# Second rates one slab earlier, the last sums inside the last slab, reloads in parts on SP, two slab copies of each turn on ACT: the RWKV projections of a hybrid diffusion step

## The reference

```python
xx = 0.5 * (prev + nxt) - h
xs = h[:, :, None, :] + xx[:, :, None, :] * p['rwkv_mu'][j]
rkvg = jnp.einsum('bsmd,mde->bsme', xs[:, :, :4], p['rwkv_w_in'][j])     # r, k, v, g
lw = decay0 + einsum(tanh(xw @ decay1), decay2)      # two directions
icl = sigmoid(icl0 + einsum(xa @ icl1, icl2))        # two directions
k_dir = k[:, :, None] * (1.0 + (icl - 1.0) * p['rwkv_k_a'][j])
bonus = (sum over a head of (r * k_dir * r_k)) * v, summed over the two directions
out = ((y + bonus) * silu(g)) @ p['rwkv_w_out'][j]   # y: the scan, a later phase
```

## Time and profile before

| what | value |
|---|---|
| median of 3 runs | 5470.27 us (5454.3 to 5471.65) |
| the profiled execution | 5479.65 us |
| its span | 5477.9 us |
| granted TensorE clock, mean | 0.919 |
| busy share of the span | PE 84%, PEld 71%, DVE 47%, ACT 35%, POOL 7% |

### The profile page before, as it was taken

One profiled execution on the slowest core, in us unless ns is written; L12 is line 12 of the kernel. 1 busy time (PEld: TensorE's weight loads), 2 busy tenths in 40 slices (PEclk: granted clock), 3 DMA queues, 4 the chain that ended last, 5 costly groups with the idle time before them and its releaser, 6 DMA issues. The chain is left out here.

```text
span 5477.9 us, 151392 instructions
## 1 busy us (share of the span) xinstructions
PE 4581.2 (84%) x68388; PEld 3876.7 (71%) x68388; DVE 2569.9 (47%) x4055; ACT 1943.1 (35%) x3694; POOL 362.7 (7%) x134
## 2 busy tenths in 40 slices
PE   3799868898887869888888599878998689889966
PEld 0488758888885745446667499876887588888846
DVE  0542436766664323136664432326324476667642
ACT  0542223444445123136663200026422244444441
POOL 0011100000000100000001022110111000000001
PEclk7899988999989879989999799989999899989988
DMA  9134573322226000000000011112446632323251
GB/s 405 44 113 134 153 201 107 85 79 77 80 75 148 31 30 27 27 6 1 1 1 28 16 43 42 35 57 69 121 124 175 202 88 71 84 71 84 62 150 58
DMA packets 624676, 466.63 MB, mean 85 GB/s; under 512 B 27456, under 2 KB 600256, under 8 KB 619712
## 3 DMA queue, kind: packets, MB, share of 16 engines
q1 hardware_dynamic: 451200, 370.05, 22.1%
q10 hardware_dynamic: 172864, 87.30, 5.7%
HBM read 333.28 MB, written 123.99 MB: 83 GB/s over the span
## 5 line engine op out<-in xcount | busy, mean ns | idle before, releaser
L417 PE MATMUL ps<-big_r,stage_r 128*128 128x384 f32 x3072 | 625.8, 338 | 95.9 <-DVE big_r L404 89.7
L623 PE MATMUL ps<-big_r,stage_r 128*128 128x384 f32 x2976 | 646.0, 352 | 25.9 <-DVE big_r L842 25.9
L417 PEld LDWEIGHTS ps<-big_r,stage_r 128*128 128x128 f32 x3072 | 546.0, 190 | 104.8 <-issue 89.4
L623 PEld LDWEIGHTS ps<-big_r,stage_r 128*128 128x128 f32 x2976 | 530.1, 191 | 105.4 <-issue 55.0
L1175 PE MATMUL ps<-arena 64*64 64x32 f32 x11520 | 438.6, 226 | 19.3 <-issue 17.8
L396 POOL TENSOR_TENSOR w_slab_r<-w_slab,stage_r 128x1024 fp32r<-128x1024 f32 x64 | 192.1, 3002 | 3763.2 <-DVE stage_r L380 3763.2
L1175 PEld LDWEIGHTS ps<-arena 64*64 64x64 f32 x11520 | 403.1, 143 | 29.8 <-issue 22.1
L417 PE MATMUL ps<-big_r,w_slab_r 128*128 128x384 f32 x1536 | 351.3, 336 | 0.0
L623 PE MATMUL ps<-big_r,w_slab_r 128*128 128x384 f32 x1488 | 344.7, 339 | 0.0
L368 PE MATMUL ps<-arena,w_slab 128*128 128x384 f32 x864 | 294.3, 502 | 27.0 <-DVE arena L1849 24.1
L1489 DVE COPY_PREDICATED arena<-arena,ps 128x128 f32<-128x128 uint32 x720 | 193.9, 325 | 183.0 <-PE ps L1149 181.8
(11 more groups left out here) (209 smaller groups left out, 7791.6 us busy)
## 6 DMA issues: line engine op xcount, KB each, us to landing
w_slab<-in_w SPq DMA_DIRECT2D x150, 512.0 KB, 3.5
scan_in<-x_resid ACTq DMA_DIRECT2D x112, 576.0 KB, 4.9
arena<-in_w_ada SPq DMA_DIRECT2D x24, 2048.0 KB, 27.8
arena<-scan_in SPq DMA_DIRECT2D x144, 320.0 KB, 3.8
arena<-scan_in SPq DMA_DIRECT2D x288, 128.0 KB, 3.8
arena<-scan_in SPq DMA_DIRECT2D x144, 192.0 KB, 4.0
arena<-scan_in SPq DMA_DIRECT2D x44, 576.0 KB, 7.8
arena<-scan_in ACTq DMA_DIRECT2D x36, 576.0 KB, 10.9
```

What stands on the lines that cost most here:

```text
L417: mm = pe.matmul(g.ps[:, bank + c, 0:CW], w[:, k * P:(k + 1) * P], x[:, k, c * CW:(c + 1) * CW], start=k == i == 0, stop=k == NB - 1 and i ...
L623: mm = pe.matmul(g.ps[:, 3 * s + c, 0:CW], w[:, k * P:(k + 1) * P], x[:, k, chunk(c)], start=k == i == 0, stop=k == NB - 1 and i == 2)
```

## The change

The icl rates of block b + 1 move from gate slab 27 + b to gate slab 26 + b, so the first gate slab holds rates(9) (after k-blocks 3, 5 and 7) and the last gate slab none. The sums of the blocks 6 and 7 both stand inside the last gate slab. The product buffer is doubled (`prod`, one of them `kk[1]`). The reloads all go to SP, k and r apart from v, the first two as soon as their part of `xx` is free. DVE's `products` is split: the sum of the two rates (`rate_sums(b)`) goes ahead, and the rest stands behind the slab copy. At each turn the copies of the first two slabs of the new matrix go from DVE to ACT (`turn`, `high_slab_of` on ACT).

```diff
-    prod = g.big[0][:, 0, :]
+    prod = [kk[1], g.big[0][:, 0, :]]
-    rates_in.update({GATE + b: NB + b for b in range(1, NB)})
+    rates_in.update({GATE + b: NB + b + 1 for b in range(NB - 1)})
...
+            def load_kr(b):
+                sp.wait_ge(stored[b % 2], 16 * (5 + b // 2))
+                if b >= 2:
+                    sp.wait_ge(p_ok, b - 1)
+                else:
+                    sp.wait_ge(xs_ok, 3 * NB + 3 * b + 2)
+                for k, arr in enumerate((A_K, A_R)):
+                    sp.dma_start(tiled(back[b % 2][k]), blocks(b, arr)).then_inc(kr_in[b % 2], 16)
+            def load_v(b):
+                sp.wait_ge(stored[b % 2], 16 * (9 + b // 2))
+                if b >= 2:
+                    sp.wait_ge(bonus_ok, CH * (b - 1))
+                else:
+                    sp.wait_ge(xs_ok, 3 * NB + 3 * b + 3)
+                sp.dma_start(tiled(back[b % 2][2]), blocks(b, A_V)).then_inc(v_in[b % 2], 16)
...
                 elif n > GATE:
                     b = n - GATE
+                    if b + 1 < NB:
+                        load_kr(b + 1)
                     store_gate(b - 1)
+                    if b + 1 < NB:
+                        load_v(b + 1)
                     store_bonus(b - 1)
...
+                    at = (3, 5, 7) if n == GATE else (1, 3, 5)
+                elif n == W_RWKV - 1:
+                    between = {j_: (lambda q=NB - 2 + i // CH, c=i % CH: sums(q, c),) for i, j_ in enumerate((1, 2, 3, 5, 6, 7))}
...
+            def high_slab_of(n):                      # on ACT
+                act.wait_ge(slab_in[n % 2], 16 * (n // 2 + 1))
+                act.wait_ge(proj_done, n - 1)
+                A.copy(g.stage_r[:, n % 2, 0:D], g.slab[:, n % 2]).then_inc(turn_ok, 1)
+            def turn(m):
+                high_slab_of(first[m])
+                for k in range(NB):
+                    high_rows(m, k)
...
+            high_slab_of(GATE + 1)
+            for b in range(NB):
+                if b < NB - 1:
+                    for c in range(CH):
+                        rates(NB + b + 1, c)
                 gate(b)
-                if b + 1 < NB:
-                    act.wait_ge(bonus_ok, CH * b)
-                    for i, arr in enumerate((A_K, A_R, A_V)):
-                        act.dma_start(tiled(back[(b + 1) % 2][i]), blocks(b + 1, arr)).then_inc(back_in[(b + 1) % 2], 16)
...
                 if m == 5:
                     if b:
-                        products(b - 1)
+                        rate_sums(b)
+                    weighted_keys(b)
+                    if b:
                         gated(b - 1)
                         high_slab_of(n + 1)
+                    products(b)
+                    if b:
                         for c in range(CH):
                             bonuses(b - 1, c)
-                    weighted_keys(b)
```

More of the change, by code:

```diff
@@ L566, in _ @@
                 if n == GATE:
[L567 to L571, removed]
+                    for b in range(2):
+                        load_kr(b)
+                        load_v(b)
                 elif n > GATE:
                     b = n - GATE
+                    if b + 1 < NB:
+                        load_kr(b + 1)
                     store_gate(b - 1)
+                    if b + 1 < NB:
+                        load_v(b + 1)
                     store_bonus(b - 1)
+            store_bonus(NB - 1)
             store_gate(NB - 1)
-            store_bonus(NB - 1)
             for s in range(2):
@@ L664, in sums @@
                 bank_free(("sum", b, c))
-                pe.matmul(g.ps[:, bank(("sum", b, c)), 0:CW], g.head_ones[:, :], prod[:, chunk(c)], start=True, stop=True).then_inc(sum_mm, 1)
+                pe.matmul(g.ps[:, bank(("sum", b, c)), 0:CW], g.head_ones[:, :], prod[b % 2][:, chunk(c)], start=True, stop=True).then_inc(sum_mm, 1)
             lora_down(0)
@@ L678, in _ @@
                 elif n in rates_in:
-                    between = {j_: (lambda u=rates_in[n], c=c: rates(u, c),) for c, j_ in enumerate((1, 3, 5))}
+                    at = (3, 5, 7) if n == GATE else (1, 3, 5)
+                    between = {j_: (lambda u=rates_in[n], c=c: rates(u, c),) for c, j_ in enumerate(at)}
                     if n > GATE:
                         between.update({j_: (lambda q=n - GATE - 1, c=c: sums(q, c),) for c, j_ in enumerate((2, 4, 6))})
+                elif n == W_RWKV - 1:
+                    between = {j_: (lambda q=NB - 2 + i // CH, c=i % CH: sums(q, c),) for i, j_ in enumerate((1, 2, 3, 5, 6, 7))}
                 slab(n, m, between)
-            for c in range(CH):
-                sums(NB - 1, c)
         @block.scalar
@@ L772, in _ @@
                 if b == NB - 1:
-                    for k in range(NB):
-                        high_rows(3, k)
+                    turn(3)
                 elif b:
@@ L783, in _ @@
                 elif b == NB - 1:
-                    for k in range(NB):
-                        high_rows(4, k)
+                    turn(4)
                 elif b:
@@ L789, in _ @@
                 copy_out(RCP + b)
+            high_slab_of(VAL + 1)
             for b in range(NB):
                 if b == NB - 1:
-                    for k in range(NB):
-                        high_rows(5, k)
+                    turn(5)
                 elif VAL + b in rates_in:
@@ L812, in _ @@
             for n in range(KEY + 1, W_RWKV):
-                pool.wait_ge(high_ok, n - 2)
+                turned = [first[m] + i for m in (3, 4, 5) for i in range(2)]
+                if n in turned:
+                    pool.wait_ge(turn_ok, turned.index(n) + 1)
+                else:
+                    pool.wait_ge(high_ok, n - KEY - sum(t < n for t in turned))
                 nc.gpsimd.tensor_tensor(g.slab_r[:, n % 2], g.slab[:, n % 2], g.stage_r[:, n % 2, 0:D], op=ALU.subtract).then_inc(low_ok, 1)
@@ L855, in transition @@
             def transition(m, extra):
-                n = first[m]
                 rows_of(m, 0)
@@ L946, in _ @@
                     high_slab_of(n + 1)
+                if n == VAL + NB - 2:
+                    dve.wait_ge(kk_st[1], 64)
+                    rate_sums(0)
                 if KEY < n < RCP or n == RCP + 1:
@@ L956, in _ @@
                     dve.wait_ge(xx_ok, NB)
-            products(NB - 1)
-            gated(NB - 1)
             for c in range(CH):
                 bonuses(NB - 1, c)
+            gated(NB - 1)
             dve.wait_ge(bonus_ok, CH * NB)
```

45 lines of the change are left out of this document (21 added, 24 removed).

## The result

The changed kernel takes 5496.5 us (median of 7 runs, 5480.3 to 5526.4), the kernel before 5460.4 in its 7 runs: ratio 1.0079 [1.0046, 1.0112]. It is slower by 0.8%: 43 us by the ratio, 36 by the two medians.

The account below looks back on a forecast made before the run. The prediction took PE to bound the changed phase, with the next slab's landing deciding when PE may go on. Five terms summed to +14.8 us per pass, +29.6 for two, giving 5500 us; own range 5488 to 5515.

Parts of the forecast that it names:

- Gate slabs, +27.7: Slabs 28 to 32: PE waits longer behind the late slab copy, 26.2 us a slab instead of 20.65, +27.7 us per pass.
- Copy at 9.17: Slabs 28 to 32: DVE's slab copy still starts 9.17 us after the slab's start, when the slab has landed.
- L910 at 3.3: Slabs 28 to 32: a DVE instruction behind the slab copy collides with POOL's subtraction and costs 3.30 us.
- Clock 1.9: Slabs 28 to 32: PE's longer wait lowers the clock and costs 1.9 us more per slab (ends 0 and 2.5).
- The other rate that I gave with the forecast: DMA at fixed 2 us and 436 GB/s: 2.9 MB through about 3.3 us earlier, the sum near zero.
- Slab 26, +2.6: First gate slab, now with rates(9): PE waits for ACT's sigmoid behind its copies, +2.6 us per pass (0 to +4).
- Slab 27, -4.3: Wait for products(0) goes, but rates(9)'s store lands late and delays the next sigmoid; -4.3 us per pass (-9 to 0).
- Tail, -8.2: Last gate slab and tail, with no rates and six sums: 23.4 to 23.6 us, -8.2 us per pass (-9 to -6).
- Turns, -3.0: Turns to receptance and value: DVE starts later and ends 1 to 3 us earlier; -3.0 us per pass together (-5 to +2).
- the slab lands in time: Rival: gate slabs' load lands at 5 to 5.6 us, the wait falls to some 2.7; about 5440 us, chance 0.20.
- Clock or collision missing: Rival: gate slabs have the wait, but not full clock loss or POOL collision; 5460 to 5481 us, same, chance 0.26.
- Does not bite: Rival: PE's waits move, gate slabs stay at 20.6 us, only slab 27 and tail gain; 5444 us, chance 0.08.

Follow-up runs that it names:

- e1: Changed kernel, but in gate slabs DVE does the three bonus products right behind the slab copy, before the rest of products; ratio 0.9985 to the kernel before.
- e3: Changed kernel, but POOL's subtraction for the next slab waits until DVE's products are done; ratio 1.0072 to the kernel before.
- e4: Changed kernel, but SP issues v's reload one slab later, behind the weight slab's load; ratio 1.0044 to the kernel before.
- e10: Changed kernel with the edits of e3 and e4 together; ratio 1.0005 to the kernel before.
- e7: e2, but SP holds back block 2's reloads in slab 27 until the stores of rates(9) have landed; ratios 0.9881 and 0.9892 to the kernel before.
- e6: e2 with the last block's three sums behind the last slab again; ratio 0.9902 to the kernel before.
- e5: e2 with the six slab copies at the turns back on DVE; ratio 0.9927 to the kernel before.
- e2: Changed kernel, but DVE does products and the first bonus product ahead of the slab copy; ratios 0.9922 and 0.9909 to the kernel before.

## Why the prediction was right, step by step

The forecast (slower, 5500) holds: the time is 5496.5. The reason holds too, but its sum was too small: +14.8 us a pass against +20.4. That the two times are only 3.5 us apart is luck: the rise was 30 forecast against 43 by the ratio, and the kernel before, whose median was 5470.3 when I forecast, has 5460.4 in these runs.

The five terms as measured add up to the whole. First pass: 30.3 + 3.6 - 2.2 - 7.8 - 3.5 = 20.4. Second pass: 28.0 + 3.4 - 0.4 - 7.6 - 3.0 = 20.4. The largest misses are slab 27 (by 2.1 and 3.9) and the gate slabs (by 2.6 and 0.3).

- **Gate slabs, +27.7.** Measured +30.3 and +28.0. Copy at 9.17: 8.9 (10.0 in slab 28). Its working does not hold in full, so that it fits so well is in part luck: I had the slab issued at its start, but SP is then busy issuing the bonus store for 2.08 us, and issues the slab 1.8 us late; the copy comes 7.4 us after that issue in the mean, and came 8.9 us after it before. L910 at 3.3: 3.38 in each of ten. (I had it last until POOL had finished; it ends 1.2 us after POOL does, at 680.26 against 679.05.) Wait 6.3: 6.3. Clock 1.9: 26.46 - 17.72 - 6.32 = 2.4, near the upper end of 2.5; the granted clock fell to 0.83 and 0.86, where I had said about 0.9. e1, e3, e4 and e10 confirm the chain of landing, copy, two instructions, collision and bonus product. The bare slab is 17.72, not 18.0.
  The other rate that I gave with the forecast is from the Trainium skill, DMA: Bandwidth & Descriptors (Anatomy of one DMA): a fixed 2 us and 436 GB/s. The page fits this to a single DMA that GpSimd issues, while these are several at once, issued by SP and ACT, so it was the wrong row to take. My working by it was off as well: as an estimate, 2.88 MB take 6.6 us at that rate against 10.1 at 285 GB/s, and with 2 us fixed in place of my 0.6 the copy would come 2.1 us earlier, not 3.3, at 7.1. It came at 8.9, and from 665.0 to the copy at 675.4 the queues moved 298 GB/s in the mean.
- **Slab 26, +2.6.** From slab 24's copy-out to slab 27's start 611.6 - 576.2 = 35.4, before 612.3 - 580.5 = 31.8: +3.6; in the second pass +3.4.
- **Slab 27, -4.3.** Measured -2.2 and -0.4. The step is right (a store behind the slab and two reloads), the size is not: I had 5 for PE's wait and 2 for the clock, and they are 6.68 and 27.04 - 17.72 - 6.68 = 2.6. e7 shows both the mechanism and what it costs.
- **Tail, -8.2.** -7.8 and -7.6; it takes 24.05 and 24.6. By e6 it isn't where the sums stand.
- **Turns, -3.0.** -3.5 and -3.0, of which the copies on ACT are 2.6 and 2.5 by e5.

Rival "the slab lands in time": the copy started at 8.9, above its limit of 7. "Clock or collision missing": both were there; the clock was 0.83 to 0.86. "Does not bite": five slabs took 134 us. What I failed to say is how cheap the way out was: the change's own aim, a slab without waits, is reached by moving `products` and the first bonus product ahead of the slab copy (e2), and is then worth 0.8 to 0.9% instead of costing 0.8%.

The Trainium skill, SBUF — State Buffer (SBUF: two separate sides), says that DVE with two SBUF inputs and POOL reading SBUF exclude each other for the whole instruction. The trace agrees: L910, with two SBUF inputs, takes 3.38 beside POOL and 1.36 without it (e3), while L923, with one input in PSUM, takes 0.56 even where it starts in the middle of POOL's subtraction (e2, slab 29):

```profile
668.82 0.56 DVE L923 TENSOR_TENSOR arena<-ps,arena 128x384 f32<-128x384 f32 x1 [1.93 <-PE ps L682]
...
666.97 2.38 POOL L843 TENSOR_TENSOR w_slab_r<-w_slab,stage_r 128x1024 fp32r<-128x1024 f32 x1 [14.14 <-DVE stage_r L852]
```

## What to carry to other kernels

On an in-order engine, put what the bounding engine waits for ahead of anything that waits for a DMA; a transfer that lands late then costs nothing, as long as it lands before its own user needs it (here 8.8 us into a slab of 17.72). When work is moved behind such a wait, price the wait, each instruction behind it, its collision with whatever the same event releases, and the clock afterwards. And weigh a change by the length of its phase, for a span can hide 40 us in stages that it does not touch.

## What the runs showed of the hardware

- Issuing takes the queue's engine longer when much is under way: in the changed kernel the slab's issue on SP took 0.34 us ahead of slab 27, after 4 us in which the queues moved nothing, and 2.7 to 3.5 in the slabs 28 to 32, behind the bonus store. In the kernel before it took 0.9 to 1.6 there.
- A DVE instruction with one SBUF input can also be held by POOL: L907, 0.81 alone, took 2.95 where it started together with POOL's subtraction (changed kernel, slab 26). In the gate slabs, where it starts 0.16 us ahead of POOL, it keeps its 0.81, and POOL's subtraction takes 2.85 instead of the 2.36 of e1.

```profile
603.93 2.95 DVE L907 TENSOR_SCALAR extra<-extra,chan 128x1152 f32<-128x1152 f32 x1
...
603.92 2.34 POOL L843 TENSOR_TENSOR w_slab_r<-w_slab,stage_r 128x1024 fp32r<-128x1024 f32 x1 [19.36 <-ACT stage_r L759]
```

- After a wait the matmuls run slow (1.65 us for four instead of 0.92), but not each time, and the length of the wait does not decide it. PE's rows of e1, then of e3:

```profile
714.22 1.65 PE L674 MATMUL ps<-x_resid 64*128 64x384 f32 x4 [2.57 <-DVE arena L923]
736.16 0.92 PE L674 MATMUL ps<-x_resid 64*128 64x384 f32 x4 [2.68 <-DVE arena L923]
```

```profile
724.13 1.65 PE L674 MATMUL ps<-x_resid 64*128 64x384 f32 x4 [4.30 <-DVE arena L925]
748.19 0.92 PE L674 MATMUL ps<-x_resid 64*128 64x384 f32 x4 [4.15 <-DVE arena L925]
```

- Without waits in the slab the granted clock over the slabs 28 to 32 is 1.00 (e2). A slab's length less 17.7 and the wait is what the clock cost. It does not simply grow with the wait: e4 waits longer than e3 and loses less. The two clocks are those of the first and the second pass.

| | wait a slab, us | granted clock | cost, us |
|---|---|---|---|
| e1 | 2.3 | 0.97, 0.95 | 0.8 |
| e10 | 2.8 | 0.92, 0.98 | 0.9 |
| e3 | 4.3 | 0.89, 0.87 | 2.1 |
| e4 | 4.8 | 0.92, 0.92 | 1.7 |
| changed | 6.3 | 0.83, 0.86 | 2.4 |

- A store of two 576 KB tiles has landed 5.9 us after its issue began if only the slab is issued close to it (e7), and after 10.8 with the slab and two reloads (changed kernel, slab 27).
